# Four modulation slices moved out of a linear-attention mixer's projections, and its in-chunk products placed between the state steps

## The reference

```python
def gla_chunk_scan(q, k, v, g, s0):            # one direction, chunks of 64
    def step(s, inp):
        b = cumsum(gc); b_end = b[:, -1]
        q_dec = qc * exp(b)
        scores = where(causal, q_dec @ (kc * exp(-b)).T, 0)
        o = scores @ vc + q_dec @ s            # in-chunk part + part from the state
        s = exp(b_end) * s + (kc * exp(b_end - b)).T @ vc
        return s, o
# mixer
q, k, v, r, glr = split(h @ w_in)
o = head_rms_norm(o_forward + flip(o_backward), norm_g)   # over 256 values per head
y = (o * silu(r)) @ w_out
# block
mod = silu(c) @ mod_w + mod_b                  # 6 vectors of 1024: 12 slices of 512 columns
x = x + gate1 * rms_norm(y, norm_g[1])
h = modulate(rms_norm(x, norm_g[2]), shift2, scale2)
x = x + gate2 * rms_norm(swiglu(h), norm_g[3])
```

## Time and profile before

| | |
|---|---|
| runs | 1334.08, 1330.63, 1333.95 us; median 1333.95 |
| profiled execution | 1330.89 us; span of the profile 1329.1 us |
| TensorE busy | 1238.1 us (93%), mean granted clock 0.965 |
| VectorE busy | 699.2 us (53%) |
| ScalarE busy | 527.8 us (40%) |
| transfers | 208.64 MB, mean 157 GB/s |

### The profile page before, as it was taken

The page is one execution under the profiler, slowest core; times in us unless marked ns, Lnnn a source line. Parts: engine busy times, 40 slices in busy tenths (PEclk is TensorE's granted clock), DMA queues, the critical chain, the costliest instruction groups (busy, mean ns, idle before and its releaser), DMA issues.

```text
span 1329.1 us, 18536 instructions
## 1 busy us (share of the span) xinstructions
PE 1238.1 (93%) x7339; PEld 1040.6 (78%) x7343; DVE 699.2 (53%) x905; ACT 527.8 (40%) x722; POOL 34.2 (3%) x50
## 2 busy tenths in 40 slices
PE   4899997889999889899999999999999988999997
PEld 1477785389999866584898998999999974798996
DVE  1577335264555420433555555677777763546554
ACT  2752221253433420343433335555555532434332
POOL 2000010000000150000000000000000000000000
PEclk9999999999999989779999999999999987999999
DMA  9568660466665420511545553755555352555510
GB/s 326 197 223 306 240 204 18 130 204 190 189 181 172 155 76 0 208 46 64 204 176 194 187 156 95 186 139 139 139 137 139 93 208 77 214 191 189 189 64 32
DMA packets 200701, 208.64 MB, mean 157 GB/s; under 512 B 5723, under 2 KB 166758, under 8 KB 200454
## 3 DMA queue, kind: packets, MB, share of 16 engines
q1 hardware_dynamic: 197536, 201.61, 47.2%
q0 software_dynamic: 1296, 3.97, 1.1%
q10 hardware_dynamic: 1814, 2.30, 0.5%
HBM read 206.81 MB, written 2.00 MB: 157 GB/s over the span
## 4 chain that ended last, share of the span: by engine, by line
PE 86%; DVE 7%; DMA 3%; ACT 2%; issue 2%; DVEq 0%; SPq 0%; ACTq 0%
PE bank L1723 18%; PE bank L1724 18%; PE bank L1725 18%; PE bank L1678 6%; DMA weight_pool<-in_mod_w_dram 2%; PE bank L1528 2%; PE bank L1530 2%; PE bank L1529 2%; PE bank L1782 2%; PE bank L1841 2%; PE bank L1858 1%; PE bank L1975 1%; PE bank L1485 1%; PE bank L1965 1%; PE bank L1790 1%
## 5 line engine op out<-in xcount | busy, mean ns | idle before, releaser
L1723 PE MATMUL bank<-hT_high,mlp_up_high 128*128 128x256 f32 x512 | 145.2, 284 | 1.5 <-DVE hT_low L1295 1.5
L1724 PE MATMUL bank<-hT_low,mlp_up_high 128*128 128x256 f32 x512 | 144.9, 283 | 0.0
L1725 PE MATMUL bank<-hT_high,mlp_up_low 128*128 128x256 f32 x512 | 144.8, 283 | 0.0
L1723 PE MATMUL bank<-od_w_high,hT_high 128*128 128x384 f32 x384 | 132.7, 346 | 1.6 <-DVE hT_low L1295 1.4
L1725 PE MATMUL bank<-od_w_high,hT_low 128*128 128x384 f32 x384 | 128.7, 335 | 0.0
L1724 PE MATMUL bank<-od_w_low,hT_high 128*128 128x384 f32 x384 | 128.4, 334 | 0.0
L942 DVE TENSOR_TENSOR mlp_down_low<-weight_pool,mlp_down_high 128x2048 fp32r<-128x2048 f32 x32 | 73.3, 2290 | 59.1 <-ACT mlp_down_high L576 59.1
L1723 PE MATMUL bank<-hT_high,ffn_up_high 128*128 128x256 f32 x352 | 99.7, 283 | 2.7 <-DVE hT_low L942 2.7
L1723 PEld LDWEIGHTS bank<-hT_high,mlp_up_high 128*128 128x128 f32 x512 | 98.1, 192 | 3.3 <-issue 2.4
L1723 PE MATMUL bank<-mlp_down_high,hidden_high 128*128 128x512 f32 x256 | 99.9, 390 | 0.0
L1724 PE MATMUL bank<-mlp_down_low,hidden_high 128*128 128x512 f32 x256 | 99.9, 390 | 0.0
(11 more groups left out here) (284 smaller groups left out, 2510.3 us busy)
## 6 DMA issues: line engine op xcount, KB each, us to landing
weight_pool<-in_mlp_w_dram SPq DMA_DIRECT2D x64, 1024.0 KB, 7.5
weight_pool<-in_od_w_in_dram SPq DMA_DIRECT2D x72, 512.0 KB, 5.2
weight_pool<-in_mod_w_dram SPq DMA_DIRECT2D x24, 1024.0 KB, 8.3
weight_pool<-in_ffn_w_in_dram SPq DMA_DIRECT2D x44, 512.0 KB, 5.2
weight_pool<-in_gla_w_in_dram SPq DMA_DIRECT2D x12, 1024.0 KB, 7.6
weight_pool<-in_ffn_w_out_dram SPq DMA_DIRECT2D x22, 512.0 KB, 6.0
weight_pool<-in_gla_w_out_dram SPq DMA_DIRECT2D x2, 2048.0 KB, 10.8
weight_pool<-in_ev_w_in_dram SPq DMA_DIRECT2D x4, 1024.0 KB, 6.6
```

Source lines behind the costliest of these rows:

```text
L1723: mm(out_, left[0], right[0], start=start, stop=False, **flag)
L1724: mm(out_, left[0], right[1], start=False, stop=False, **flag)
L1725: return mm(out_, left[1], right[0], start=False, stop=stop, **flag)
```

## The change

Slices 8 to 11 leave the projections. Slices 8 and 9 run on PE after the last state step; their turning and summing come before `turn_mixed`. Slices 10 and 11 run after `out_product`; their copies lie on ACT between `y_stats` and `norm_stats`, their sums on DVE between `gated_update` and `norm_scale`. The gate rows are made one at a time: the mixer's during the normalisation, the other after the feed-forward part. The in-chunk products are cut into three pieces between the state steps; the zero products go, the last `from_states` closes the sums. The squares of the normalisation are taken per bank without a sum, and DVE sums them. `turn_mixed` goes by token tile. The weights of slice 10 go to a part of `work`, those of slice 11 over the first output weights, and the feed-forward weights 2 and later queue behind them.

```diff
-LATE_AFTER = {0: (4,), 1: (5,), 3: (6,), 4: (7,), 5: (8,), 6: (9,), 7: (10,), 9: (11,)}
+LATE_AFTER = {0: (4,), 1: (5,), 5: (6,), 7: (7,)}
...
+        for i in (8, 9):
+            for half in range(2):
+                L["mod", i, half] = plan(f"mod{i}_{half}", 4096 * (i - 8) + 2048 * half,
+                                         [(0, (4, 512), mod_v[:, 4 * half:4 * half + 4, i, :])], ("mod_rows", i + 1),
+                                         ring=f"w_ring{2 * (i - 8) + half}")
...
+            if f == 2:
+                for half in range(2):
+                    L["mod", 11, half] = plan(f"mod11_{half}", 8192 + 2048 * half,
+                                              [(0, (4, 512), mod_v[:, 4 * half:4 * half + 4, 11, :])], ("mod_rows", 12),
+                                              ring=f"w_ring{(4, 0)[half]}")
...
@@ SP @@
+            for i in (8, 9):
+                for half in range(2):
+                    fetch(L["mod", i, half])
             for i in range(2):
                 fetch(L["go", i])
+            for e in L["ffn"][:2]:
+                fetch(e)
+            sp.wait_ge(s["og_ready"], 2)
+            sp.dma_start(view(work, 16384, KD, 512), mod_v[:, :, 10, :]).then_inc(s["mod_loaded"], 16)
+            for half in range(2):
+                fetch(L["mod", 11, half])
...
@@ ACT @@
+            for b in range(4):
+                act.activation(work[:, 12288 + 512 * b:12800 + 512 * b], bank[b][:, :], ACT.Square).then_inc(s["o_sq"], 1)
             for t in range(NT):
-                for h in range(GH):
-                    chain(act.activation(work[:, 20480 - 5 * 1024:20480 - 5 * 1024 + GDV],
-                                         bank[2 * t + h // 2][:, GDV * (h % 2):GDV * (h % 2) + GDV], ACT.Square,
-                                         accum_out=stat[:, 16 + 4 * t + h:17 + 4 * t + h]))
-            act.activation(stat[:, 24:32], stat[:, 16:24], ACT.Sqrt, bias=eps, scale=1.0 / GDV).then_inc(s["o_std"], 1)
+                act.wait_ge(s["o_sum"], 2 * t + 2)
+                act.activation(stat[:, 24 + 4 * t:28 + 4 * t], stat[:, 16 + 4 * t:20 + 4 * t], ACT.Sqrt, bias=eps, scale=1.0 / GDV)\
+                   .then_inc(s["o_std"], 1)
+            mod_copy(8)
+            mod_copy(9)
...
+            def late_stats(t):
+                y_stats(0, t)
+                if t:
+                    mod_copy(10)
+                    mod_copy(11)
...
@@ DVE @@
-            for b in range(4):
-                dve.wait_ge(s["rows_ps"], b + 1)
-                dve.tensor_copy(rows[:, b // 2, 512 * (b % 2):512 * (b % 2) + 512], bank[4 + b][:, :]).then_inc(s["rows_ready"], 1)
+            for b in range(4):
+                square_sums(b)
...
             for t in range(NT):
+                dve.wait_ge(s["o_std"], t + 1)
+                chain(dve.reciprocal(stat[:, 8 + 4 * t:12 + 4 * t], stat[:, 24 + 4 * t:28 + 4 * t]))
                 for h in range(GH):
...
                 ins.then_inc(s["og_ready"], 1)
+                if t == 0:
+                    gate_copy(0)
+            mod_reduce(8)
+            mod_reduce(9)
+            dve.wait_ge(s["mod_cols"], 10)
...
+            def late_update(t):
+                gated_update(0, t)
+                if t:
+                    mod_reduce(10)
+                    mod_reduce(11)
...
@@ DVE, after the feed-forward units @@
+            dve.wait_ge(s["mod_cols"], 12)
+            eff_gate(4, 5, 3)
+            gate_copy(1)
             norm_scale(3, res, xn, before=lambda t: gated_update(1, t))
...
@@ PE @@
-            for j in range(4):
-                if j < 3:
-                    state_updates(j + 1)
-                from_states(j)
-            pe.wait_ge(s["zero_ready"], 1)
-            for b in range(4):
-                ins = mm(bank[b][:, 0:512], zero[:, 0:P], zero[:, :], start=False, stop=True, skip_group_check=True)
-            ins.then_inc(s["o_ps"], 1)
+            in_chunk(0, range(4))
+            state_updates(1)
+            from_states(0)
+            in_chunk(1, (0, 1))
+            state_updates(2)
+            from_states(1)
+            in_chunk(1, (2, 3))
+            state_updates(3)
+            from_states(2)
+            from_states(3)
+            mod_slice(8)
+            mod_slice(9)
...
+            gate_rows(0)
+            pe.wait_ge(s["rows_ready"], 2)
+            mod_turn(8)
+            mod_turn(9)
+            pe.wait_ge(s["mod_cols"], 10)
+            turn_mixed(0, og, "og_ready")
             out_product(0, [("go", 0), ("go", 1)], ogT)
+            mod_slice(10)
+            mod_slice(11)
+            mod_turn(10)
+            mod_turn(11)
+            pe.wait_ge(s["mod_cols"], 12)
             turn_tokens(2, xn)
...
             ffn_round(FF_LOOPS * FF_RING, FFC - FF_LOOPS * FF_RING, last=True)
+            gate_rows(1)
```

More of the change, by code:

```diff
@@ L423, in fetch, with fetch_ring @@
                     sp.dma_start(view(pool, e.at + off, *sh), src).then_inc(e.sem, 16)
-            def fetch_ring(bundles, ring, parts_of):
-                for e in bundles[:ring]:
+            def fetch_ring(bundles, ring, parts_of, first=0):
+                for e in bundles[first:ring]:
                     fetch(e)
@@ L1128, in _, with square_sums, gate_copy @@
                     ins.then_inc(s["state_ready"], 1)
+            def square_sums(b):
+                dve.wait_ge(s["o_sq"], b + 1)
+                dve.tensor_reduce(stat[:, 16 + 2 * b:18 + 2 * b], work[:, 12288 + 512 * b:12800 + 512 * b].rearrange("p (h d) -> p h d", h=2),
+                                  AX, ALU.add).then_inc(s["o_sum"], 1)
+            def gate_copy(n):
+                for b in range(2):
+                    dve.wait_ge(s["rows_ps"], 2 * n + b + 1)
+                    dve.tensor_copy(rows[:, n, 512 * b:512 * b + 512], bank[6 + b][:, :]).then_inc(s["rows_ready"], 1)
             for b in range(4):
-                dve.wait_ge(s["rows_ps"], b + 1)
-                dve.tensor_copy(rows[:, b // 2, 512 * (b % 2):512 * (b % 2) + 512], bank[4 + b][:, :]).then_inc(s["rows_ready"], 1)
-            dve.wait_ge(s["o_std"], 1)
-            chain(dve.reciprocal(stat[:, 8:16], stat[:, 24:32]))
+                square_sums(b)
             dve.wait_ge(s["gr_ready"], 8)
             for t in range(NT):
+                dve.wait_ge(s["o_std"], t + 1)
+                chain(dve.reciprocal(stat[:, 8 + 4 * t:12 + 4 * t], stat[:, 24 + 4 * t:28 + 4 * t]))
                 for h in range(GH):
@@ L1639, in from_states, with in_chunk @@
                                  qd[:, z, h, CHUNK * cl:CHUNK * cl + CHUNK], states[:, j % 2, z, h, :],
-                                 start=False, stop=False, skip_group_check=True)
-                ins.then_inc(s["inter_ps"], 1)
+                                 start=False, stop=(j == 3), skip_group_check=True)
+                ins.then_inc(s["o_ps" if j == 3 else "inter_ps"], 1)
+            def in_chunk(h, banks):
+                for b in banks:
+                    for z in range(2):
+                        ins = mm(bank[b][:, GDV * h:GDV * h + GDV], sT[:, z, b % 2, 2 * h + b // 2, :],
+                                 vG[:, 2 + b // 2, GDV * (2 * (b % 2) + h):GDV * (2 * (b % 2) + h) + GDV], start=(h == 0 and z == 0), stop=False,
+                                 skip_group_check=True)
@@ L1643, in _ @@
             context_state(0)
             context_state(1)
-            for t in range(NT):
-                for u in range(2):
-                    for h in range(2):
-                        for z in range(2):
-                            mm(bank[2 * t + u][:, GDV * h:GDV * h + GDV], sT[:, z, u, 2 * h + t, :],
-                               vG[:, 2 + t, GDV * (2 * u + h):GDV * (2 * u + h) + GDV], start=(h == 0 and z == 0), stop=False,
-                               skip_group_check=True)
-            for j in range(4):
-                if j < 3:
-                    state_updates(j + 1)
-                from_states(j)
@@ L1666, in turn_mixed @@
+            state_updates(2)
[6 more added lines that the diff above has]
+            mod_slice(9)
+            def turn_mixed(n, src, ready=None):
+                for t in range(NT):
+                    if ready:
+                        pe.wait_ge(s[ready], t + 1)
+                    for b in range(4):
+                        for k in (2 * b, 2 * b + 1):
                             ins = pe.transpose(bank[4 + b][:, 256 * (k - 2 * b) + P * t:256 * (k - 2 * b) + P * t + P],
@@ L1667, in turn_mixed @@
                                                src[:, t, P * k:P * k + P], ident)
-                    ins.then_inc(s["ogT_ps"], 1)
+                        if t == NT - 1:
+                            ins.then_inc(s["ogT_ps"], 1)
             def out_product(n, keys, srcT):
```

75 lines of the change are left out of this document (36 added, 39 removed).

## The result

The changed kernel takes 1320.10 us (median of 6 runs, 1316.82 to 1324.11); the kernel before, run beside it, takes 1331.28 (6 runs, 1329.21 to 1334.08). The ratio is 0.9915, 95% interval 0.9893 to 0.9936: faster, by more than the 0.3% that a measurement tells. The forecast was 1322. A later series gave 1318.07 (7 runs, 1315.86 to 1325.40) against 1332.87 (17 runs), ratio 0.9883, interval 0.9864 to 0.9903. The profiled execution took 1319.19 us; its span is 1317.4, against 1329.1 before: 11.7 us, where the sum said 11.2.

The account below looks back on a forecast made before the run. TensorE was taken as the bound, 86% of the chain that ended last. Terms 9.0 + 3.7 + 0.25 + 0 - 1.75 = 11.2 us gave 1319.7 from 1330.89, 1322.8 from 1333.95; forecast 1322, range 1317 to 1328.

Parts of the forecast that it names:

- 1. Slices out of the projections: Projections: four slices with turnings leave at 2.49 us each, 10.0 us, less a 0.95 us stall; net gain 9.0.
- the stall: Projections, chunk 4's third tile: TensorE waits for VectorE to copy q's third tile after the scan, costing 0.95 us.
- The rival of the r chunks: Projections: the split becomes the bound, chunk 10's low part 6.7 us late; gain 4.5, time 1329, chance 0.10.
- 2. Products between the steps: State steps: in-chunk products fill waits, cycle 5.7 us and TensorE-bound, zero products gone; gain 3.7 us.
- 3. The normalisation: Normalisation, from X, when the sums stand: output product at X+12.1 instead of X+12.35; gain 0.25 us, at half rate loss 1.05.
- The choice of full rate: Normalisation: with no gap ahead above 1.7 us, TensorE's turning of `og` was taken at full rate, not 0.216 us each.
- the rival: Half rate at normalisation and border: transposes stay at 0.216 us, 1.3 and 0.5 us more; gain 9.4, 1324, chance 0.15.
- 5. The border: From E, the output product's end: second scaling near E+8.2 instead of E+7.55, four full-rate turnings; net 0, at half rate 0.5 lost.
- the rival that everything adds up (5.0): Border: new TensorE, ScalarE and VectorE pieces add up instead of overlapping, up to 5.0 us lost; gain 6.2, 1327, chance 0.12.
- 6. The second gate: After the feed-forward part: second gate's rows and VectorE's copies lie on the path, nothing hides them; cost 1.75 us.
- 7. SP's queue: SP's transfer queue: feed-forward weight 2 waits for slice 11, goes out at E+3.8, needed at E+19.7; no cost.
- The rival's price: Feed-forward weights starve: each microsecond past E+19.7 stops TensorE; sign turns 11 us past the longest landing; 1336 and more, chance 0.04.

Follow-up runs that it names:

- VectorE's order mended: The changed kernel with VectorE's copies of q's third tile moved before the second scan: 1318.56 us (4 runs), ratio 0.9893 to the kernel before.
- combined kernel: The changed kernel plus q's third tile copied before the scan, in-chunk products 6, 6, 4, second gate's rows in the last feed-forward unit: 1317.16 us, ratio 0.9878.

## Why the prediction was right, by its own steps

**1. Slices out of the projections: 8.66 for 9.0.** With VectorE's order mended the stage is 80.43 against 90.47 before, so four slices are worth 10.04, 2.51 each for 2.49. The term that was mis-sized is the stall: 0.95 in the sum, 1.08 as a wait, 1.38 by the experiment. Two slices put back cost 4.07 for 4.03 by the prediction's prices, but that they meet is luck: a stall larger by 0.4 and a wait for VectorE behind slice 9 that the sum didn't have cancel. The mechanism is shown. The rival of the r chunks didn't come in the changed kernel, where no wait stands in them; the wait behind slice 9, 0.33 us with two slices back, shows how near it was.

**2. Products between the steps: 3.57 for 3.7.** The cycle is 5.73, as forecast (5.7). From the silu to the end of the last `from_states` the sum had 37.88, and it is 37.95. Of its parts, 2.6 are the products and 1.0 the zero products.

**3. The normalisation: 0.53 for 0.25.** X is 207.33. The sums ended at X+3.1, the first four multiplies at X+4.9, the copies at X+6.2, the rest of `og` at X+8.0, the two sums at X+8.6; forecast X+3.1, 4.95, 6.35, 8.2, 9.0. Each later step of VectorE was rated 0.04 to 0.2 too dear, and the last one most: the two sums took 0.6 where the sum had 0.75 and a handover. Instructions in a row overlap a little: four reductions of 0.69 take 2.46 together. The choice of full rate held in this trace. It is, however, not the program's property: of ten traces with this same order of work in the normalisation, eight have the turning at 1.97 us and two at 3.26 and 3.63. Half rate cost 1.0 and 1.4 there, where the prediction said 1.3. Two of ten doesn't speak against the 0.15 given to the rival, and as this place decides about a tenth of the gain, the forecast stood either way.

**5. The border: 0.27 gained for 0.** The reading that the residual is late anyway was right, and the rival that everything adds up (5.0) is refuted by the kernel without slices: without them this place is slower by 0.27, or quicker by 0.19 at most. The square and scaling of the second tile ended at E+7.9, forecast 8.2, without slices at E+7.5. The Trainium skill, TensorE: Matmul & The Clock Gate, Part 1, says that activity releases the half rate and idleness brings it back. What the prediction left open was whether slices of 32 columns count. With them the turning at the border takes 2.3 us in nine traces of eleven, without them 3.33 after 6.11 idle, which agrees. So filling the gap mostly keeps the rate up; whether products of 32 columns count as much as wider ones, or only the shorter wait does it, was not separated. As in the normalisation, full rate was the likelier case and not a certain one.

**6. The second gate: 1.70 lost for 1.75**, and 1.78 by leaving the rows out. "Nothing hides it" was true for the place where they stood. In the middle of the last down product they cost 0.4.

**7. SP's queue: nothing, as said.** In the changed kernel weight 2 went out at 250.49 and ScalarE used it at 266.27 without a wait. The rival's price, "each microsecond past E+19.7 would stop TensorE", was wrong as a mechanism and nearly right as a number: about 4 us are free, but the lower clock behind the stop took back 2.2 of them. 8.1 us late cost 6.7, and the kernel was still 5.9 us faster than before. The sign would turn at a lateness of some 14 us, an estimate from 8.1 and 5.9 more at one for one; the prediction had 11.

**The sum.** 11.2 us off the 1331.28 of before's runs in the same series is 1320.1, the median measured; that they meet to a tenth is luck, as the interval is some 3 us to either side. The forecast of 1322 stood on the choice between before's profiled run and its median, then 1333.95; that choice, not the sum, is its 1.9 us. In the later series the difference of medians is 14.8, 3.6 more than the sum; the stages of the trace taken there don't show it, and the runs of one kernel spread by 9.5.

## What to carry to other kernels

Work taken out of a full stretch of TensorE pays its whole price, less the first stall of whoever was just in time there; look for that engine's next deadline and reorder it along with the move. Work put into a gap must be weighed against the engine that makes the gap: in the normalisation, where `og` could be turned only after the slices' sums, they cost 1.06 us; at the border their copies and sums held the last scaling by 0.4 us, and TensorE, kept going, mostly won it back in the turning. Read such prices from stages cut at the same instructions: here they repeat to 0.05 us where the clock is the same, while whole runs of one kernel spread over 9.

## What the runs showed of the hardware that I had not expected

The granted clock of one place is not fixed by the program. Sixteen transposes after the same gaps (0.79 and 1.29 us) and the same work took 1.97 us in eight traces, 3.26 and 3.63 in two. What differed in those two was not found. In one of them (the second gate's rows left out) the projections were unlike the changed kernel's as well: the stage took 83.39 us instead of 81.81, and so it did, 83.41, with the zero products back, though neither edit touches it. Busy time by stretch there (columns as above), first in the changed kernel, then with the second gate's rows left out:

```profile
88.00:98.00 10.00, 8.14 (x52) 8.01 (x53) 9.90 (x9) 2.38 (x3) 0.00 (x0) 0.83 0.65 244
98.00:110.00 12.00, 10.92 (x49) 8.67 (x48) 11.93 (x10) 5.64 (x6) 0.00 (x0) 1.00 0.27 87
```

```profile
88.00:98.00 10.00, 7.29 (x56) 6.72 (x55) 9.86 (x12) 3.88 (x3) 0.00 (x0) 1.00 0.80 295
98.00:110.00 12.00, 10.15 (x38) 7.91 (x37) 11.93 (x10) 4.69 (x5) 0.00 (x0) 0.86 0.24 84
```

A spell at the lower clock falls into either of two neighbouring stretches, and where it falls later it costs 1.6 us more. VectorE is busy throughout in both. In two other traces (rows in the last unit, weights held back) both stretches have 1.00, and the stage takes 81.78 and 81.76: TensorE then comes earlier to q's third tile and waits 1.8 to 1.9 us for VectorE instead of 1.08. So the earlier spell costs nothing, as TensorE would wait for VectorE behind it anyway; the later one lies behind that wait and counts. But in the other trace with a slow turning, the combined kernel's, these two stretches read 0.83 and 1.00 like the changed kernel's, so this is not the cause of the slow turning; it stays open.

A stop of TensorE for 4.19 us was followed by 5 us at 0.50 of the clock, which cost 2.2 us beside the stop. A stop is thus dearer than its length.

A weight of three transfers counts as landed with its last, here 8.4 us after its first issue; the median landing of single transfers around it is 7.3, and the third went out 1.0 us after the first.
